# The last two gate units of the first attention as joined products of 512 and 256 columns

## The reference, cut to what matters

```python
xn = rmsnorm(x, norm_attn[l])
proj = xn @ w_in[l]
rq, rk, rv, rg, sq, sk, sv, ga, gb = jnp.split(proj, split_points, axis=-1)
...
ret = group_norm(retention(rq, rk, rv), ret_group_norm) * jax.nn.silu(rg)
y_a = ret @ w_branch_ret[l]
...
sb = stick_breaking(sq, sk, sv)
y_b = sb @ w_branch_sb[l]
mixed = jax.nn.sigmoid(ga) * y_a + jax.nn.sigmoid(gb) * y_b
x = x + mixed @ w_out[l]
```

## Time and profile before

| | us |
|---|---|
| median of 3 runs | 1983.34 (1983.23 to 1983.45) |
| the profiled execution's own time | 1983.32 |
| its span | 1981.5 |
| TensorE (PE) busy | 1973.2 |
| GpSimd (POOL) busy | 1424.8 |
| VectorE (DVE) busy | 1282.0 |
| ScalarE (ACT) busy | 1043.9 |

### The profile page before, as it was taken

One profiled execution on the slowest core, in us unless ns is written; L12 is line 12 of the kernel. 1 busy time (PEld: TensorE's weight loads), 2 busy tenths in 40 slices (PEclk: granted clock), 3 DMA queues, 4 the chain that ended last, 5 costly groups with the idle time before them and its releaser, 6 DMA issues.

```text
span 1981.5 us, 38996 instructions
## 1 busy us (share of the span) xinstructions
PE 1973.2 (100%) x13942; PEld 1763.5 (89%) x13942; DVE 1282.0 (65%) x2183; ACT 1043.9 (53%) x1364; POOL 1424.8 (72%) x604
## 2 busy tenths in 40 slices
PE   9999999999999999999999999999999999999998
PEld 8899898888888888888889899888888888888887
DVE  5256387864776899953336748886467789994333
ACT  6556555565555544445447665556555554444444
POOL 7667878888777878854448757888877787884442
PEclk9999999999999999999999999999999999999999
DMA  8444545555555555566555345555555555555553
GB/s 271 163 139 149 178 162 186 189 183 189 179 170 174 176 169 171 174 209 206 194 188 180 124 143 170 191 188 185 181 178 169 174 176 170 175 174 180 201 191 127
DMA packets 100467, 351.44 MB, mean 177 GB/s; under 512 B 12464, under 2 KB 15408, under 8 KB 100272
## 3 DMA queue, kind: packets, MB, share of 16 engines
q1 hardware_dynamic: 99680, 348.61, 52.9%
q10 hardware_dynamic: 720, 1.92, 0.3%
HBM read 349.44 MB, written 1.05 MB: 177 GB/s over the span
## 4 chain that ended last, share of the span: by engine, by line
PE 99%; DMA 0%; DVE 0%; ACT 0%; POOL 0%; SPq 0%; issue 0%
PE ps L1268 24%; PE ps L1334 12%; PE ps L1269 12%; PE ps L1336 12%; PE ps L1337 6%; PE ps L1335 6%; PE ps L739 4%; PE ps L741 4%; PE ps L740 4%; PE ps L896 4%; PE ps L1260 3%; PE ps L898 2%; PE ps L933 1%; PE ps L823 1%; PE ps L1244 1%; PE ps L1146 1%
## 5 line engine op out<-in xcount | busy, mean ns | idle before, releaser
L657 POOL TENSOR_TENSOR wlo<-ring,whi 128x1024 fp32r<-128x1024 f32 x565 | 1370.3, 2431 | 515.0 <-ACT whi L1694 427.7
L1694 ACT ACTIVATE whi<-ring 128x1024 fp32r<-128x1024 f32 x536 | 566.6, 1060 | 718.2 <-PE ps L1337 387.2
L1268 PE MATMUL ps<-hboth,whi 128*128 128x512 f32 x2048 | 714.6, 395 | 0.0
L1269 PE MATMUL ps<-hboth,wlo 128*128 128x256 f32 x2048 | 567.7, 277 | 0.0
L1268 PEld LDWEIGHTS ps<-hboth,whi 128*128 128x128 f32 x2048 | 384.1, 188 | 87.3
L1334 PE MATMUL ps<-whi,shi 128*128 128x512 f32 x1024 | 404.2, 395 | 0.0
L1336 PE MATMUL ps<-wlo,shi 128*128 128x512 f32 x1024 | 400.4, 391 | 0.0
L1269 PEld LDWEIGHTS ps<-hboth,wlo 128*128 128x128 f32 x2048 | 384.6, 188 | 0.0
L1337 PE MATMUL ps<-whi,slo 128*128 128x256 f32 x1024 | 286.7, 280 | 0.0
L1335 PE MATMUL ps<-whi,slo 128*128 128x256 f32 x1024 | 285.7, 279 | 0.0
L1336 PEld LDWEIGHTS ps<-wlo,shi 128*128 128x128 f32 x1024 | 192.2, 188 | 43.4
(11 more groups left out here) (335 smaller groups left out, 2893.7 us busy)
## 6 DMA issues: line engine op xcount, KB each, us to landing
ring<-in_weights SPq DMA_DIRECT2D x651, 512.0 KB, 3.3
act<-in_const SPq DMA_DIRECT2D x11, 198.0 KB, 3.5
act<-in_const SPq DMA_DIRECT2D x8, 192.0 KB, 4.9
xres<-in_x SPq DMA_DIRECT2D x4, 256.0 KB, 5.2
act<-in_keys ACTq DMA_DIRECT2D x1, 1024.0 KB, 4.7
ring<-in_weights SPq DMA_DIRECT2D x2, 256.0 KB, 5.0
act<-in_fgain ACTq DMA_DIRECT2D x1, 512.0 KB, 3.5
out<-act SPq DMA_DIRECT2D x1, 512.0 KB, 2.6
```

What stands on the lines that cost most here:

```text
L657: pool.tensor_tensor(wlo[:, j, :], ring[:, j, :], whi[:, j, :].bitcast(F32), ALU.subtract)\
L1268: pe.matmul(bank(b), whi[:, j, c], hboth[:, :, kc, :], start=kc == 0, stop=False, skip_group_check=True)
L1269: mm = pe.matmul(bank(b, 0, S), wlo[:, j, c], hhi[:, kc, :], start=False, stop=kc == KC - 1, skip_group_check=True)
L1694: eng.activation(whi[:, j, :], ring[:, j, :], ACT.Copy).then_inc(hi_ready[j], 1)
```

## The change

Units 24 and 25 are computed with `joined_columns`, unit 24 in banks 2 and 3, unit 25 in banks 0 and 1. TensorE waits for `stay_ready` = 4 ahead of the first and for `arg_ready` = 4 ahead of the second. Two semaphores are new. ScalarE, when a unit's products are in, copies the low parts into `gate_part` (in the memory of `tmpA`, used for the heads' rotation before), for unit 25 only when VectorE has added unit 24's. VectorE adds in place in PSUM, waits for that add, and multiplies by `R` from there.

```diff
+JOINED_GATE_BANK = {24: 2, 25: 0}
...
+        gate_part = tmpA[:, :, 0:S]
...
-            def joined_columns(i, b, free, left=None):
-
-                for half in range(HALVES):
+            def joined_columns(i, b, free, left=None, parts=(0, 1)):
+
+                for half in parts:
...
+                        elif i in JOINED_GATE_BANK:
+                            free = (stay_ready, PAIRS) if i == 24 else (arg_ready, PAIRS)
+                            joined_columns(HALVES * i, JOINED_GATE_BANK[i], [free] * TT, parts=parts)
...
+                        if i in JOINED_GATE_BANK:
+                            b = JOINED_GATE_BANK[i]
+                            if i > 24:
+                                eng.wait_ge(gate_joined, i - 24)
+                            eng.activation(gate_part, ps[:, b:b + 2, S:2 * S], ACT.Copy).then_inc(gate_parted, 1)
...
-                        eng.wait_ge(slot_used, HALVES * (i + 1))
-                        eng.tensor_tensor(gateT[name][:, off // P:off // P + 2, :], bank(4 + i % 2).rearrange("p (j t) -> p j t", j=2),
-                                          R, ALU.mult).then_inc(gate_scaled, 1)
+                        if i in JOINED_GATE_BANK:
+                            b = JOINED_GATE_BANK[i]
+                            product = ps[:, b:b + 2, 0:S]
+                            eng.wait_ge(gate_parted, i - 23)
+                            eng.tensor_tensor(product, product, gate_part, ALU.add).then_inc(gate_joined, 1)
+                            eng.wait_ge(gate_joined, i - 23)
+                        else:
+                            product = bank(4 + i % 2).rearrange("p (j t) -> p j t", j=2)
+                            eng.wait_ge(slot_used, HALVES * (i + 1))
+                        eng.tensor_tensor(gateT[name][:, off // P:off // P + 2, :], product, R, ALU.mult).then_inc(gate_scaled, 1)
```

More of the change, by code:

```diff
@@ L478, in block_program @@
         so_copied = sem("sb_out_copied")
+        gate_parted = sem("gate_low_part_copied")
+        gate_joined = sem("gate_parts_joined")
         ret_parted = sem("ret_low_part_copied")
```

## The result

The changed kernel takes 1987.02 us, median of 19 runs (1985.28 to 1988.24); the kernel before, in 19 runs beside it, 1983.12 us (1982.64 to 1984.29). The ratio is 1.0019, with a 95% interval of 1.0012 to 1.0025: slower by 3.9 us, about at the bound of 0.2% set ahead. The forecast was 1985.9 with a range of 1985.3 to 1988.1. The wait that it described is there to a tenth of a microsecond. What it took for the less likely case, that the clock falls in this wait, is what happened in the profiled run and, by their times, in most of the others, at a smaller price than it gave. The median lies above the forecast's own range of 1985.4 to 1986.7, and inside the wider one only because that was stretched over the clock's case.

What follows compares the result with a forecast made beforehand. TensorE, busy 1973.2 of 1981.5 us and never waiting after its first 8 us, bounds the kernel. u=1 starts 2.49 us later, saving included, plus 0.1 restart: 1983.3 + 2.6 = 1985.9 us, range 1985.3 to 1988.1.

Steps and rivals of the forecast that it cites:

- The wait that it described: TensorE ahead of stick-breaking branch unit u=1: stands still 2.7 us until VectorE has scaled unit 25.
- the forecast's own range: Whole kernel, if the clock holds and no second wait comes: 1985.4 to 1986.7 us; chance 0.77.
- the clock's case: Rival: TensorE's clock falls in the pause before u=1, 2.1 us more, 1988.0 us; chance 0.14.
- TensorE's work: Units 24 and 25 on TensorE: one instruction fewer per group saves 0.107 us a unit, 0.21 both.
- Unit 24's way out: Unit 24's copy, add, multiply: nobody waits; ScalarE's rounding of m=53 and all behind start 0.38 us later, hidden.
- Unit 25's way out: Unit 25's copy queues on ScalarE until 188.65, multiply done 190.70; u=1 starts 190.76, 2.49 us later than before.
- the restart: TensorE's first matmuls of u=1 behind the wait: a slower second start, 0.1 us added.
- What is late next: Slots m=54 to 57 and work behind the copy: later, but cover of 4 us or more, no second wait.
- The clock: TensorE's clock in the pause before u=1: forecast to hold; its fall was a rival, chance 0.14.
- My pause: TensorE idle from 188.2 to 190.76, 2.5 us, against a clock fall 2.77 us after the kernel's last matmul.
- Its price: Cost if the clock falls before u=1: slow start of at least 4.2 us, half lost, 2.1 us.

Runs made afterwards that it cites:

- e2: Changed kernel with only unit 24 joined, unit 25 as before the change; 1982.85 us, ratio 0.9998 to the kernel before.
- e3: Changed kernel with only unit 25 joined, unit 24 as before the change; 1986.43 us, ratio 1.0014 to the kernel before.
- e5: Changed kernel with unit 25's copy on ScalarE ahead of the rounding of m=54, still behind the gb Sigmoid; 1984.84 us, ratio 1.0009 to the kernel before.
- e1: Changed kernel with ScalarE's Sigmoid of gb moved behind unit 25 in the schedule; 1982.82 us, ratio 0.9998 to the kernel before.
- e6: Changed kernel with the copies of the low parts made by VectorE, nothing new on ScalarE; 1982.88 us, ratio 1.0001 to the kernel before.
- e7: Kernel before, nothing joined; only u=1 on TensorE waits for the Sigmoid of ga instead of unit 25's scaling; 1987.55 us, ratio 1.0021 to the kernel before.
- e4: Changed kernel with ten spare 512-column products on TensorE ahead of u=1, result unused; 1985.85 us, ratio 1.0012 to the kernel before.
- e8: e3 with eight spare 512-column products filling TensorE's pause; 1985.39 us, ratio 1.0012 to the kernel before.

## Why the prediction came out as it did

- *TensorE's work.* From the start of unit 23's second half to u=0's start, 15.45 us before and 15.26 after: 0.19 us saved, 0.21 forecast. With one unit joined (e2, e3) it is 0.08 and 0.10.
- *Unit 24's way out.* Hidden, as forecast (e2). ScalarE's rounding of m=53 started at 180.14 instead of 180.29; 0.11 of these 0.15 us are the start of the span, since this execution was that much earlier from unit 23 on.
- *Unit 25's way out.* Copy 188.50 (forecast 188.65), multiply done 190.53 (190.70), u=1 at 190.68 (190.76), all of them with the same 0.11 us of an earlier start in them; the pause 2.71 (2.70), the restart, read in e3 and e5, 0.08 (0.1). One term was too small: TensorE starts 0.15 us after VectorE's multiply ends, not the 0.06 that the earlier trace rows had at the kernel's start (0.14 in e3 and e5). The steps ahead of it came 0.06 us sooner than forecast, which hides most of that. That this comes from ScalarE's order is shown from three sides: e1 moves what stood ahead and e6 moves the copy to another queue, and the wait goes; e5 takes one rounding out, and the pause shortens by that rounding.
- *What is late next.* Nothing behind it waited in the changed kernel's trace. One price was off and did no harm: the retention multiply took 3.92 us, not 2.29 (last section).
- *The clock.* Here the weighing failed. The step was: "My pause ends some 0.2 us short of that", a yardstick of 2.77 us taken from the one pause at the end of the kernel. In the changed kernel's trace the clock fell after 2.3 us; 16 of 19 runs lie at 1986.4 or above and three at 1985.7 or below, and the forecast's 1985.9 is near what these three give. Pauses by the records and runs that lay in the higher group: 1.60 us, none of 11 (e5); 2.14, six of 11 (e3); 2.55, 16 of 19; 2.83, eight of 11 (e7). One reading of one pause could not give that spread. By run times alone the groups are a reading. That the higher one is the clock is shown for the changed kernel and e7, each by a trace of a run in that group, and by e4, where the filled pause gives the full clock and the shorter time; for e3 it is inferred from its traced lower run and from e8.
- *Its price.* Forecast at 2.1 us from the start of the kernel, which had at least 4.2 us at the slow pace. Measured 1.46 with the restart, and 1.39 against e4: the slow stretch lasted from 190.44 to 193.84, and the first 0.24 us of it fell into the pause. Of the 3.16 us from 190.68 to 193.84 it cost 1.38, so 0.44 of the time and not half. The start's row could not give this price: it shows a slow pace of another length, and the granted clock reads 1.00 there (0 to 9 us), so that this pace was the clock's low level was assumed and not read.

The weight given to the fall of the clock, 0.14, was too small. The Trainium skill (TensorE: Matmul & The Clock Gate, Part 1) warns of idle gaps between bursts of matmuls; the traces here agree, with a granted clock of 0.50 behind the pauses of 2.55 and 2.83 us.

None of the versions is faster than the kernel before by more than these runs can tell. The saving that the change was able to give, 0.19 us, is 0.01% of the time; e1, e2 and e6 lie 0.3 to 0.4 us below before in the medians, within their intervals.

## What to carry to other kernels

When a result gets an extra step on another engine, read that engine's queue at the moment of need, not its busy share: ScalarE was busy 53% of the time, yet unit 25's result came 4.2 us later than before (190.53 against 186.28) by steps that take 2.1 us, because a Sigmoid and a rounding for later work stood ahead. On a kernel in which TensorE never waits, count a new pause as the pause and a stretch at half clock besides: here pauses of 2.1 us and more brought it, by the run times, in many of the runs, for some 1.4 us each, and one of 1.6 us in none. And compare the most that a change can save with the wait that it risks before building it: here 0.2 us against 2.7.

## What the runs showed of the hardware

- The clock need not fall inside a pause. It fell 0.24 us before the work resumed in one trace and 0.8 us after it had resumed in another (e7), and by its run times one kernel has executions with the fall and without it.
- The restart behind a wait costs 0.08 us: the second matmul starts 0.19 to 0.20 us behind the first, not 0.12 (e3, e5, e7). It isn't the wait's alone: in the kernel before, u=2 follows the turns without a wait and has the same 0.20:

```profile
192.82 0.36 PE L739 MATMUL ps<-sbhi,whi 128*128 128x256 f32 x1
193.02 0.28 PE L740 MATMUL ps<-sblo,whi 128*128 128x256 f32 x1
```
- A VectorE operation on SBUF and a GpSimd one that run together stretch the one that came second. Before, VectorE's multiply of 128x2048 began at 180.72 and took 2.29 us, and GpSimd's low half, begun at 181.05, took 4.22. After, GpSimd's began first, at 181.27, and took 2.40, and VectorE's, from 181.90, took 3.92:

```profile
181.27 2.40 POOL L661 TENSOR_TENSOR wlo<-ring,whi 128x1024 fp32r<-128x1024 f32 x1 [1.86 <-ACT whi L1462]
```

  The additions and multiplies with one operand in PSUM kept their 0.69 and 0.70 us beside GpSimd's work (189.11 and 189.84 above, while GpSimd worked from 188.67).
